# POOL's subtraction for a weight slab in four operations of 128x256 instead of one of 128x1024

## The reference

```python
def first_block(x, c, ctx, ...):            # for each of 2 layers, on x and on ctx
    h = modulate(x, g_pre[l], shift, scale)
    rk, rv, dk, dv, rq, rg, dq, dg, mu, mv, mg, mlog = split_cols(h @ w_in[l], IN_SIZES)
    rq, rk, dq, dk = apply_rope(...)        # x only, not ctx
    ... retention, differential attention, gated MLP ...
    y = g_ret * (o_ret @ w_bo[0]) + g_mlp * (o_mlp @ w_bo[1]) + g_diff * (o_diff @ w_bo[2])
    x = x + gate * rms_norm(y @ w_o, g_post[l])

def second_block(x, ...):                   # for each of 2 layers
    proj = _rmsnorm(x, g_mix) @ w_in
    ... three attentions, one over keys that an index score selects ...
    x = x + (gated sum of the three @ w_branch) @ w_out
    x = x + square(relu(_rmsnorm(x, g_mlp) @ w_up)) @ w_down
```

## Time and profile before

| | us |
|---|---|
| median of 3 runs | 2117.91 |
| lowest and highest | 2117.65, 2120.18 |
| the profiled execution, whole | 2118.09 |
| its span, first to last instruction | 2115.9 |
| PE busy in it | 1954.5 |
| POOL busy in it | 1385.0 |
| DVE busy in it | 790.8 |

### The profile page before, as it was taken

One profiled execution on the slowest core, in us unless ns is written; L12 is line 12 of the kernel. 1 busy time (PEld: TensorE's weight loads), 2 busy tenths in 40 slices (PEclk: granted clock), 3 DMA queues, 4 the chain that ended last, 5 costly groups with the idle time before them and its releaser, 6 DMA issues.

```text
span 2115.9 us, 26201 instructions
## 1 busy us (share of the span) xinstructions
PE 1954.5 (92%) x9488; PEld 1569.0 (74%) x9488; DVE 790.8 (37%) x1211; ACT 1099.7 (52%) x1573; POOL 1385.0 (65%) x573
## 2 busy tenths in 40 slices
PE   6998999969899979789989999999999989999997
PEld 3776887856667758667868777788888867778886
DVE  3234224955305469532244342341111632251111
ACT  3545644525533654355445694644445486555443
POOL 3754787924467759346868744388887944478885
PEclk9999999989999999999999999999999999999999
DMA  9643465623486546234654533265554633335553
GB/s 359 201 131 110 143 189 165 189 66 105 166 270 208 176 118 191 78 109 132 190 167 140 155 100 98 75 196 180 188 179 137 203 103 93 106 129 181 187 180 118
DMA packets 170814, 328.63 MB, mean 155 GB/s; under 512 B 12384, under 2 KB 13536, under 8 KB 170464
## 3 DMA queue, kind: packets, MB, share of 16 engines
q1 hardware_dynamic: 167968, 320.49, 49.1%
q10 hardware_dynamic: 2752, 6.84, 0.9%
HBM read 326.24 MB, written 1.05 MB: 155 GB/s over the span
## 4 chain that ended last, share of the span: by engine, by line
PE 40%; issue 30%; POOL 24%; ACT 3%; DVE 2%; POOLq 1%; DMA 0%; DVEq 0%; ACTq 0%
POOL wlo L467 24%; PE G L1438 9%; PE G L1440 8%; PE G L1439 8%; PE A L1438 3%; PE A L1439 3%; PE A L1440 3%; DVE work L1332 1%; ACT t L540 1%; PE A L1492 1%; ACT whi L481 1%; PE A L1816 0%; PE A L1815 0%; PE A L1814 0%; ACT L823 0%
## 5 line engine op out<-in xcount | busy, mean ns | idle before, releaser
L467 POOL TENSOR_TENSOR wlo<-raw,whi 128x1024 fp32r<-128x1024 f32 x568 | 1381.3, 2441 | 708.5 <-ACT whi L481 703.7
L481 ACT ACTIVATE whi<-raw 128x1024 fp32r<-128x1024 f32 x568 | 599.5, 1058 | 639.8 <-PE G L1440 502.1
L1438 PE MATMUL G<-whi,hhi 128*128 128x512 f32 (+1 forms) x1648 | 661.5, 401 | 17.8 <-DVE hlo L929 11.3
L1440 PE MATMUL G<-whi,hlo 128*128 128x512 f32 (+1 forms) x1648 | 644.3, 391 | 0.0
L1439 PE MATMUL G<-wlo,hhi 128*128 128x512 f32 (+1 forms) x1648 | 644.0, 391 | 0.0
L1438 PEld LDWEIGHTS G<-whi,hhi 128*128 128x128 f32 x1648 | 313.4, 190 | 99.4 <-issue 30.7
L1440 PEld LDWEIGHTS G<-whi,hlo 128*128 128x128 f32 x1648 | 313.0, 190 | 66.4
L1439 PEld LDWEIGHTS G<-wlo,hhi 128*128 128x128 f32 x1648 | 313.7, 190 | 59.6
L1438 PE MATMUL G<-whi,ohi 128*128 128x512 f32 x240 | 95.2, 397 | 2.4 <-ACT gates L494 1.4
L1439 PE MATMUL G<-wlo,ohi 128*128 128x512 f32 x240 | 93.5, 390 | 0.0
L1440 PE MATMUL G<-whi,olo 128*128 128x512 f32 x240 | 93.5, 390 | 0.0
(11 more groups left out here) (363 smaller groups left out, 2593.6 us busy)
## 6 DMA issues: line engine op xcount, KB each, us to landing
raw<-in_w_in SPq DMA_DIRECT2D x332, 512.0 KB, 3.7
raw<-in_w_up SPq DMA_DIRECT2D x64, 512.0 KB, 3.6
raw<-in_w_down SPq DMA_DIRECT2D x64, 512.0 KB, 3.3
raw<-in_w_out SPq DMA_DIRECT2D x40, 512.0 KB, 3.7
raw<-in_w_branch_out SPq DMA_DIRECT2D x36, 512.0 KB, 3.9
modw<-in_w_mod SPq DMA_DIRECT2D x32, 512.0 KB, 3.9
raw<-in_w_branch SPq DMA_DIRECT2D x24, 512.0 KB, 3.3
modz<-in_w_mod SPq DMA_DIRECT2D x16, 512.0 KB, 10.9
```

Of the source, the lines that this page charges most:

```text
L467: pool.tensor_tensor(wlo[:, s], raw[:, s], whi[:, s].bitcast(F32), ALU.subtract).then_inc(lo_ready, 1)
L481: act.activation(whi[:, slot], raw[:, slot], ACT.Copy).then_inc(hi_ready, 1)
L1438: pe.matmul(bank, hi, whi[:, slot, kk, 0:n], start=first, stop=False)
L1440: return pe.matmul(bank, lo, whi[:, slot, kk, 0:n], start=False, stop=last)
```

## The change

The one operation of L467 becomes a loop over the two row blocks `kk` and the two halves of the 512 columns. Only the last of the four operations raises `lo_ready`, and only the first has a wait for `hi_ready` ahead of it. What is computed is the same.

```diff
@@ -464,7 +464,12 @@
             with w.loop(slabs // SLOTS, {hi_ready.name: SLOTS}) as i:
                 for s in range(SLOTS):
                     pool.wait_ge(hi_ready, w(hi_ready))
-                    pool.tensor_tensor(wlo[:, s], raw[:, s], whi[:, s].bitcast(F32), ALU.subtract).then_inc(lo_ready, 1)
+                    for kk in range(SLAB_K):
+                        for c in range(2):
+                            part = slice(c * CH // 2, (c + 1) * CH // 2)
+                            ins = pool.tensor_tensor(wlo[:, s, kk, part], raw[:, s, kk, part], whi[:, s, kk, part].bitcast(F32),
+                                                     ALU.subtract)
+                    ins.then_inc(lo_ready, 1)
```

## The result

The changed kernel is slower, by 1.2%. Its executions took 2138.20, 2142.73, 2148.84 and 2170.57 us, against 2117.65 to 2120.18 for the kernel before beside them; the longest of the four fell in a slower state that the comparison leaves out, and without it the median is 2142.73 us and the ratio to before 1.0116, with an interval of 1.0083 to 1.0148. The profiled execution is the one of 2138.20 us, with a span of 2136.0, so its trace shows 20.1 us of a loss of about 25, and the longest execution has no trace. My forecast was 2103.6 us and faster. The measured time lies inside the range that I gave, 2082 to 2152, but only because the range reached up for rival A's larger f; at the f that was measured my sum gave 2103.6, so that much is luck.

What follows compares the result with a forecast made beforehand. The prediction took PE's 2.72 us per slab as the bound, POOL a close second and DVE held to POOL's pace. From 2118.1 us, minus 25.5 gain plus 11 loss gave 2103.6 us, range 2082 to 2152.

Steps and rivals of the forecast that it cites:

- rival A: POOL becomes the bound and the kernel is slower, deciding from f = 0.17; 2133 us at f = 0.20; chance 0.33.
- f: Fixed cost of one POOL operation, three more per slab after the change; taken as 0.14 us.
- What bounds the kernel: PE at 2.72 us per slab, POOL close behind; DVE enters between POOL operations, causing PE's waits of 17.2, 10.3, 9.7 us.
- (1): POOL's time for a slab in four operations: 2.78 us, between 2.45 and 3.08.
- (2): Cost of longer slabs where POOL must catch up, in projections, merges and smaller places: 11 us.
- smaller places: Allowance within the loss for minor stretches and for DVE's more frequent entries: 3 us.
- (3): DVE enters four times as often, shortening PE's three long waits and the index scores: 9 + 5.5 + 7 + 4 = 25.5 us.
- (4): No semaphore added; `lo_ready` seen 0.4 us later per slab, covered by POOL's 4.4 us lead or already counted.
- p: POOL's undisturbed time for one slab after the change, 2.36 + 3 x 0.14 = 2.78 us.
- C: DVE gets in no more often because POOL keeps the port between operations: no gain, 2129 us; chance 0.05.
- B: The fixed cost is nearly hidden, below 0.10 us, and POOL stays under PE's pace: 2088 us; chance 0.15.
- D: Gain and loss cancel, with half of DVE's gain because the next wait is closer: 2116 us; chance 0.05.

Runs made afterwards that it cites:

- e1: The changed kernel's four pieces made 208 columns wide instead of 256, the last 48 of each quarter left out: 2072.43 us, ratio 0.978.
- e12: The changed kernel plus a wait of POOL for its own completion behind every fourth slab: 2143.35 us, ratio 1.0132.
- e5: The changed kernel plus a wait of POOL for its own completion behind every slab: 2186.39 us, ratio 1.031.
- e2: The kernel before, its one operation kept, plus a clearing of an unread buffer that fills the slab to about 2.78 us: 2150.5 us, ratio 1.0152.
- e8: The changed kernel's four pieces made 232 columns wide, 24 columns of each quarter left out: 2099.23 us, ratio 0.9904.
- e4: The kernel before with quarters only in the slabs where DVE keeps PE waiting, whole operations elsewhere, no pause: 2117.0 us, ratio 0.9987.
- e6: The kernel before with quarters only where DVE keeps PE waiting, and POOL waiting for its own completion behind each cut slab: 2102.47 us, ratio 0.9911.
- e11: The changed kernel with its four quarters in another order, column half outside and row block inside: 2153.32 us, ratio 1.0143.

## Why the prediction was wrong

*What bounds the kernel.* Right in kind. POOL's pace, DVE's entries at POOL's passages and the three waits are all as read, and e1 shows how much hung on the passages: 48 us.

*(1) The time of a slab.* Right. f was to be between 0.03 and 0.24 us, taken as 0.14. Start to start an undisturbed operation takes 0.42 us at 128 columns, 0.59 at 208, 0.64 at 232, 0.695 at 256, 1.25 at 512 and about 2.35 at 1024 elements, which is 2.16 ns for an element and 0.14 us for the operation. The Trainium skill's 4497 ns for an addition of 2048 elements (GPSIMD Engine Reference, Performance versus the Vector engine) made f 0.28 us when I set it against 2.39 us for half as many. By the line through the measured points that size takes 4.56 us, so the figure itself is within 2% of what the runs show, and the f made from it is twice the measured one. Half of the excess is these 2%; the other half is my 2.39 us, a duration read beside other work, where the line has 2.35. The value by the section's cycles per element, 0.14 us, is the one measured.

*(2) The loss, forecast 11 us, measured 38.7 in the trace.* This is the step that failed. The second block's merges (2.6 us each forecast; 3.7 and 3.2 measured) and the feed-forwards (nothing, and nothing) held. The first projection lost 7.5 us where I had 1.3, 5.5 of them at slabs 308 to 312 where DVE was shut out; the other lost 2.3. The wrong term is "with 3 us for smaller places and for DVE's more frequent entries". The first block alone lost 22.0 us outside the waits, some 5 of them by shut-outs (of 7.4 and 7.2 us, at 122 and 667).

Another 5 of the 22.0 are neither entries nor shut-outs. From slab 122 to 134 the kernel after loses 5.0 us, and e12 and e5, whose slabs are as long or longer, lose 0.4 each. What differs is PE's granted clock, 0.05 less and then 0.10 less over 35 us each, which is 5 us. Busy time by stretch there, first the kernel before, then after (columns as in rows 9):

```profile
535.00:570.00 35.00, 29.72 (x152) 23.66 (x156) 17.95 (x26) 20.12 (x28) 16.31 (x6) 0.90 0.37 120
```

```profile
500.00:535.00 35.00, 30.41 (x155) 22.61 (x153) 16.89 (x42) 19.88 (x41) 15.30 (x23) 0.95 0.34 104
535.00:570.00 35.00, 27.87 (x129) 23.08 (x130) 17.77 (x27) 20.56 (x30) 15.68 (x20) 0.80 0.26 83
```

The kernel before is granted 1.00 from 500 to 535, and so are e12 and e5, which have 0.90 behind it like the kernel before. Why after is granted less there is open.

The term failed even so: e12 has no DVE operation over 4.2 us and the clock of before in that stretch, and still loses some 17 us in the first block outside the waits. I had asked whether 40 slabs of 2.78 us fit into 113 us; they do, and e2 loses 1.3 us over slabs 48 to 108. But I had priced DVE's entries only for the stretches where DVE was the late one. An entry lengthens POOL's slab wherever it falls: the twenty slabs of the rotary stretch take 65.84 us, 10.2 more than 20 x 2.78, for 60 DVE operations, so 0.17 us each (I had 0.15, from rows 4 and 5). A slab with four entries takes 3.4 to 3.6 us beside PE's 2.72. Before the change an entry came once per slab, and POOL had 0.33 us per slab to spare for it. After, up to four come, and the spare time is -0.06 us. The mechanism was in my own rows, and I used it for the gain and not for the loss.

*(3) The gain, forecast 25.5 us, measured 18.8.* The first wait gave 9.0 against 9, which is 17.2 at the wait itself less 8.2 paid on the way; the index scores 1.8 each against 2; the last wait 3.9 against 5.5. The wait at 755.91 gave 2.3 against 7: PE's wait of 10.30 us did go, but L1136's work runs beside POOL now and PE waits for it in parts (the row at 763.96, and 4.2 us in all with its neighbours), and the slabs ahead of it came late. The agreement at the first wait is partly luck. I had PE resume 9 us earlier; it was 9.6 us late when the stage began (slab 96) and resumed 2.9 us late (443.32 against 440.44), which is a gain of 6.7. The other 2.3 us are PE's clock, which the forecast did not have. PE's transposes at the wait before, in full, where rows 3 show 26 of the 32:

```profile
440.44 6.55 PE L1480 MATMUL A<-const,z 128*128 128x128 f32 x32 [17.18 <-DVE z L1017]
```

Busy time by stretch in the 7 us from PE's resumption, before and then after (PE, PEld, DVE, ACT, POOL, clock, DMA):

```profile
440.00:447.00 7.00, 6.55 (x32) 6.34 (x32) 0.29 (x1) 4.00 (x7) 0.00 (x0) 0.55 0.00 0
```

```profile
443.00:450.00 7.00, 5.38 (x41) 4.95 (x41) 0.43 (x1) 5.23 (x10) 7.00 (x12) 1.00 0.62 171
```

After the long wait PE had a granted clock of 0.55 in this stretch, near the lower of its two levels (1.2 of 2.4 GHz), and did its 32 transposes in 6.55 us; without the wait it is granted 1.00 and does them in 3.71.

*(4) Waits.* Right, but for what no semaphore shows: the shut-outs. They came with unbroken runs of POOL's shorter operations, though not with every such run (none in e1), and the forecast has no term for them.

*The rivals.* A, POOL becomes the bound, is nearest to what happened, but by another door: I let it decide from f = 0.17, that is p = 2.87, and at p = 2.96 gave 2133 us. The kernel with 2.98 us (e5) takes 2186. From 2.57 (e8) to 2.78 the time rises from 2099.2 to 2142.7, 207 us for each us of slab (my expectations have 222, from a median with the longest execution in it), and to e5 by about as much again (43.7 us for 0.20). The shut-outs are inside these differences: in the traces they cost PE nothing in e1, 8.4 us in e8, some 11 in after and nothing in e5. The time of the kernel before is crossed near p = 2.66, or f = 0.10. My sum had 65 us for a us of p below 2.78 (2082 to 2103.6) and 160 just above. C is out (5.64 us for eight at L966), and so are B and D.

*What is shown and what not.* Shown: the passages' worth, the clock that comes with them included (e1), the own time's cost without them (e2), the entries' price per slab and when PE pays it (e1, e8, after), the shut-outs, and that a pause of POOL ends them (e4 against e6, e5, e12). Not shown apart: how the loss outside the waits divides between entries, own time and clock. Open: why a given DVE operation is shut out. The six longest (31.24 to 58.08 us) are each the first of a burst, with 7 us or more of idle time of DVE before them. Shorter ones come without it: those of 13.33 and 16.64 us (e11) and 14.81 (e8) had 0.03 us. Whether idle time makes them long was not tried. How much the shut-outs add to the median of the changed kernel is an estimate: some 11 us in its trace by the ledger (3.3 at slab 24, 2.0 at 164, 5.5 at 312), and about 10 by e12, with intervals as wide as that. The best kernel of the study that computes the whole product is e6, 0.9% under the kernel before.

## What to carry to other kernels

Where two engines keep each other out and take turns, cutting the operations of the one with the long operations gives the other its turns, but each turn taken lengthens the first one's work, and that has to be summed over every stretch where the first has nothing to spare, not only where the gain is. Cut only where somebody waits for the other engine, and check what the cut work's own time per item is against the pace that it must hold: here 0.42 us per slab turned a gain of 48 us into a loss of 25. Leave a break in the run of cut operations, and look in the trace after for single operations that last tens of times their usual length.

## What the hardware showed that I had not expected

A single DVE operation with two inputs from SBUF can be kept from the port it shares with POOL for 58.08 us, over some seventy of POOL's operations, each begun as the last ended. The Trainium skill (SBUF — State Buffer, SBUF: two separate sides) says that of a DVE operation with two SBUF inputs and a GpSimd operation that reads SBUF, whichever starts first gets the shared pair for the whole instruction and the other fully blocks. Read as ending with the one operation, that is a wait of 0.7 us here. It mostly does (0.77 us for the operation behind the 38.93), and the traces of after, e4 and e11 show that it need not. A wait of POOL for its own completion costs 0.20 us (from 2.78 to 2.98 us per slab, 0.16 of it as idle time in e5's row) and was followed by no shut-out over 4.2 us. DVE operations that read PSUM for one of their inputs were not touched in any of the traces: `e<-G,gates` of 128x512 takes 0.68 or 0.69 us before and after, beside 1.96 and 1.40 us in the mean for `y<-y,e`.
